# Token rows of a hybrid diffusion step: loaded on SP's queue behind the fourth modulation unit instead of first on ScalarE's queue

## The reference

```python
mod = (jax.nn.silu(cond) @ w_mod + b_mod)[:, None, :]
sh1, sc1, g1, sh2, sc2, g2 = jnp.split(mod, 6, axis=-1)
h = rmsnorm(x, norm1_w) * (1 + sc1) + sh1
(u_in, gate_b, gate_c, q, k, v, g_out, lr_f, lr_b,
 gate_br_conv, gate_br_gla) = jnp.split(h @ w_in, points, axis=-1)
y_conv = gate_b * conv3_rows(gate_c * u_in, conv_w, conv_b, rows, row_len)
y_gla, s_f, s_b = gla_mixer(q, k, v, g_out, lr_f, lr_b, w_decay, b_decay, gla_norm_w, s0_f, s0_b)
merged = (jax.nn.sigmoid(gate_br_conv) * (y_conv @ w_br_conv)
          + jax.nn.sigmoid(gate_br_gla) * (y_gla @ w_br_gla))
x = x + g1 * (merged @ w_out)
h2 = rmsnorm(x, norm2_w) * (1 + sc2) + sh2
x = x + g2 * moe(h2, w_router, b_router, w_gate_e, w_up_e, w_down_e, w_gate_s, w_up_s, w_down_s)
```

## Time and profile before

| | |
|---|---|
| median of three runs | 1021.3 us |
| lowest, highest | 1020.84, 1022.47 us |
| profiled execution, first to last instruction | 1021.6 us |
| TensorE busy | 929.6 us (91%) |
| VectorE busy | 365.8 us (36%) |
| ScalarE busy | 185.9 us (18%) |
| GpSimd busy | 104.1 us (10%) |
| moved by DMA | 324.25 MB, mean 317 GB/s |

### The profile page before, as it was taken

How to read it: one execution, slowest core, us unless ns; L and a number is a source line. 1 busy time by engine, 2 the same in 40 slices (tenths; PEclk the granted TensorE clock), 3 DMA queues, 4 the chain that set the end, 5 groups by cost and what they waited for, 6 DMA issues and landing times.

```text
span 1021.6 us, 12985 instructions
## 1 busy us (share of the span) xinstructions
PE 929.6 (91%) x4915; PEld 481.5 (47%) x4915; DVE 365.8 (36%) x711; ACT 185.9 (18%) x277; POOL 104.1 (10%) x205
## 2 busy tenths in 40 slices
PE   4899899999999999999999999997998897988785
PEld 0454456677555568644444444442433343433332
DVE  3309613137200325442344333333232233232256
ACT  2140320112001002202222112221111121211111
POOL 2000000000000000020212122121121121111100
PEclk9999899999999999999999999998999999999998
DMA  9745556522363359798999999999999999999994
GB/s 373 266 165 213 193 212 206 182 65 76 110 237 130 108 181 421 311 395 357 363 373 418 419 420 419 421 420 419 420 419 421 423 420 419 420 421 420 422 419 199
DMA packets 82384, 324.25 MB, mean 317 GB/s; under 512 B 10350, under 2 KB 39194, under 8 KB 52368
## 3 DMA queue, kind: packets, MB, share of 16 engines
q1 hardware_dynamic: 66864, 289.43, 71.0%
q0 software_dynamic: 10080, 24.44, 6.1%
q10 hardware_dynamic: 5376, 9.52, 2.6%
HBM read 301.52 MB, written 34.11 MB: 329 GB/s over the span
## 4 chain that ended last, share of the span: by engine, by line
PE 78%; DVE 8%; DMA 5%; issue 5%; ACT 3%; SPq 1%; DVEq 0%; ACTq 0%
PE bank L522 25%; PE bank L1680 18%; PE bank L551 13%; PE bank L1837 4%; PE bank L1824 4%; DMA arena<-expert_rows 3%; DMA arena<-in_w_mod_dram 2%; PE bank L509 2%; PE bank L1744 2%; PE bank L1864 2%; ACT arena L533 1%; PE bank L540 1%; DVE arena L536 1%; PE bank L1665 1%; PE bank L482 1%
## 5 line engine op out<-in xcount | busy, mean ns | idle before, releaser
L522 PE MATMUL bank<-arena 128*32 128x512 f32 (+2 forms) x1536 | 266.0, 613 | 35.6 <-issue 34.6
L1680 PE MATMUL bank<-arena 128*128 128x384 f32 x640 | 211.8, 492 | 4.7 <-DVE arena L1072 4.7
L522 PEld LDWEIGHTS bank<-arena 128*32 128x32 f32 (+2 forms) x1536 | 94.0, 127 | 204.7 <-issue 203.9
L1680 PEld LDWEIGHTS bank<-arena 128*128 128x128 f32 x640 | 121.8, 192 | 97.0 <-issue 9.9
L551 PE MATMUL bank<-arena 128*32 128x512 f32 (+2 forms) x768 | 131.5, 595 | 6.6 <-issue 5.9
L551 PEld LDWEIGHTS bank<-arena 128*32 128x32 f32 (+2 forms) x768 | 44.7, 123 | 70.2 <-issue 70.2
L564 ACT ACTIVATE arena<-arena 128x1024 f32<-128x1024 f32 x36 | 41.3, 1148 | 166.3 <-DVE arena L560 163.7
L556 DVE SCALAR_TENSOR_TENSOR arena<-bank,arena 128x512 f32<-128x512 f32 x36 | 27.0, 751 | 108.0 <-PE bank L551 107.9
L496 POOL DMA_INDIRECT arena<-h_rows,arena x36 | 38.4, 1067 | 240.4 <-issue 124.3
L536 DVE TENSOR_TENSOR arena<-arena,bank 128x256 f32<-128x256 f32 x36 | 21.8, 606 | 113.5 <-ACT arena L533 113.5
L533 ACT ACTIVATE arena<-bank 128x256 f32<-128x256 f32 x36 | 22.3, 619 | 204.6 <-PE bank L522 204.6
(11 more groups left out here) (246 smaller groups left out, 713.6 us busy)
## 6 DMA issues: line engine op xcount, KB each, us to landing
arena<-in_w_gate_e_dram SPq DMA_DIRECT2D x64, 1024.0 KB
arena<-in_w_up_e_dram SPq DMA_DIRECT2D x64, 1024.0 KB
arena<-in_w_down_e_dram SPq DMA_DIRECT2D x64, 1024.0 KB
arena<-in_w_mod_dram SPq DMA_DIRECT2D x24, 1024.0 KB, 8.2
arena<-in_w_in_dram SPq DMA_DIRECT2D x22, 1024.0 KB, 5.8
expert_rows<-arena SPq DMA_DIRECT2D x6, 2048.0 KB, 23.6
arena<-expert_rows SPq DMA_DIRECT2D x12, 1024.0 KB, 25.3
arena<-mod_rows_out ACTq DMA_DIRECT2D x4, 1024.0 KB, 8.2
```

Source lines behind the costliest of these rows:

```text
L522: ins = pe.matmul(bank[off:off + width, :], x_T[:, k, off:off + width], w[:, :, k, :], start=(k == 0), stop=(k == KT - 1))
L1680: ins = pe.matmul(ps[:, 0:TOK], w[:, k, P * (n % 2):P * (n % 2) + P], hT[:, k, :], start=(k == 0), stop=(k == KT - 1))
```

## The change

The two DMAs that load x leave ScalarE's program, where they were the first thing, and stand in SP's loop behind the fourth unit. The same semaphore counts them.

```diff
                 sp.dma_start(unit_view(u), unit_source(u)).then_inc(unit_in[n % UNITS], 16)
+                if u == ("mod", 0, 3):
+                    sp.dma_start(xn[:, 0, :], x_prompt[0]).then_inc(S["x_in"], 16)
+                    sp.dma_start(xn[:, 1:3, :], x_sample[0].rearrange("(t p) d -> p t d", p=P)).then_inc(S["x_in"], 16)
...
-            act.dma_start(xn[:, 0, :], x_prompt[0]).then_inc(S["x_in"], 16)
-            act.dma_start(xn[:, 1:3, :], x_sample[0].rearrange("(t p) d -> p t d", p=P)).then_inc(S["x_in"], 16)
             act.wait_ge(S["cond_in"], 32)
             act.wait_ge(S["cond_zeroed"], 1)
```

## The result

The change makes the kernel slower. The changed kernel took 1024.68 us in the median (15 runs, 1022.72 to 1027.44), and the kernel before 1021.96 us (15 runs, 1020.74 to 1024.04, the three known ones among them). The ratio is 1.0032, with a 95% interval of 1.0024 to 1.0041. So the change costs 0.14 to 0.32%, some 1.4 to 3.3 us.

The account below looks back on a forecast made before the run. The prediction took unit 7's landing at 28.8 us, set by DMA bandwidth, as the bound. Terms +0.6 (start), +0.1 (x) and +0.3 (clock) gave +1.0, a median of 1022.3 us, range 1020.7 to 1024.6.

Parts of the forecast that it names:

- What limits the stretch: First 42.64 us: the landing of unit 7 sets the first large projection, and a delay there reaches the end one to one.
- Start of the stream: SP's queue: unit 0, issued at 1.74, flows from about 3.2 us, so all that follows is 0.6 us later.
- The estimate beside it: SP's queue: from the skill's first-byte time, unit 0 would flow at 2.3 us, costing nothing or gaining a little.
- x late: Ahead of unit 7: x lands 9.5 us later, all swallowed but 0.1 us, without a reserve, if TensorE's clock is up.
- The clock: TensorE after the hole before unit 4: lower clock level, then a rise soon after x's rows are ready, costing 0.3 us.
- rival 2: TensorE stays at 1.2 GHz behind the late x; unit 7 starts over 1.4 us behind its landing; chance 0.18.
- cold and half-cold cases: TensorE behind x: lower clock throughout gives +4.3 us, 1025.6; a rise halfway gives about 1023.9 us.
- ScalarE's queue, hidden: ScalarE's later DMA issues start 9.5 us later but finish at 32.0 us, hidden by 0.9 us before the feature copies.
- Rival 3: ScalarE stuck in its queue: router issues take 8.1 us as before, +4.5 us, 1025.8 us; chance 0.08.
- Rival 1: SP's queue flows at once, so nothing shifts or 0.3 us are won: 1021.0 to 1021.3; chance 0.14, shared.
- rival 5: No effect: x does not wait for units 0 to 3 and lands near 10 us, 1021.3; shared chance 0.14.
- Rival 4: Clock luck in later matmul pieces, 2.3 us each: 1019.9 or 1024.6 us; chance 0.05 faster, 0.03 slower.

Follow-up runs that it names:

- experiment 4: Kernel before the change plus six extra 384-column products on TensorE ahead of the first large projection; 1.0036 of the kernel before.
- experiment 6: Changed kernel with x two units later, behind the sixth unit on SP's queue; 1.0074 of the kernel before.
- experiment 2: Changed kernel with x two units earlier, behind the second unit on SP's queue; 1.0018 of the kernel before.
- experiment 3: Changed kernel with x first on SP's queue, ahead of all units and behind the conditioning vectors; 1.0011 of the kernel before.
- experiment 1: Changed kernel with 12 small extra products in TensorE's idle time behind the fourth, fifth and sixth units; 1.0010 of the kernel before.
- experiment 7: Changed kernel with the two conditioning vectors moved to ScalarE's queue, x still behind the fourth unit; 1.0016 of the kernel before.
- experiment 9: Changed kernel with the conditioning vectors on ScalarE's queue and 17 small extra products in TensorE's idle time; 1.0014 of the kernel before.
- experiment 8: Changed kernel with x behind the second unit and the conditioning vectors on ScalarE's queue; 1.0001 of the kernel before.

## Why the prediction was wrong

**What limits the stretch**: right. The landing of unit 7 set the pace before, and where the first large projection was moved by 4 and by 9 us, the end moved with it, within the intervals (experiments 4 and 6).

**Start of the stream, 0.6 us**: right in kind, mis-sized. It measured 1.1 to 1.2 us (experiments 2 and 3), at or just over my upper bound of 1.1. I had let the stream run at its full rate from 3.2 us, from a reading of x's start (2.1 us) that was too early: 253 GB/s over 2 to 3 us is, at 414 GB/s, a start at 2.4. In fact the stream moved 0.09 MB from 3 to 4 us, and its 2.72 to 2.77 MB by 10 us are a full rate from 3.3 to 3.4. The simple account would have been nearer: the first large load is issued 0.92 us later, so all that follows is 0.92 us later. The estimate beside it, a flow from 2.3 us at no cost, fell.

**x late, 0.1 us**: the sum was right. I forecast x at 18.96 and its rows at 26.7; it was 19.57 and 27.3, and the difference is the stream's. With the clock up, unit 7 starts at 29.94 (experiment 1) where the landing alone gives about 30.0 (experiments 2 and 3).

**The clock, 0.3 us**: this is the step that failed. It measured 1.6 to 3.0 us: against experiment 1 the slow array cost 2.96, 1.60 and 1.84 us in three profiles of the changed kernel. I had seen the hole, the lack of a reserve, and the price of the full case, and then wrote "a rise soon after" because the gaps between units 4 and 5 were like those in which the clock had risen. But before, the rise fell into the third unit in a row with such a gap ahead of it (0.52, 0.66 and 0.64 us). After the change only unit 5 has one, and ahead of unit 4 stands the hole. The lower level lasted to 30.7 us or beyond in all three, and unit 7 started 1.5 to 2.2 us behind its landing (30.0), over the 1.4 that I had named for rival 2. Its cold and half-cold cases, to which I gave 0.18 together, are what the profiles show. (The cold case took transposes of 1.74 us, twice 0.87; at the lower level they took 1.54.) The rule of the Trainium skill that I cited (TensorE: Matmul & The Clock Gate, Part 1), that idle gaps bring the throttle back, is borne out by experiment 7 (1.07 us per unit ahead of a gap of 6.54 us, 1.93 behind it), and I gave it too little weight.

**ScalarE's queue, hidden**: right. The two issues that had taken 5.80 and 2.32 us took this:

```profile
28.94 0.81 ACTq L1500 DMA_DIRECT2D arena<-in_b_router_dram  x1
29.78 1.57 ACTq L1501 DMA_DIRECT2D arena<-in_w_router_dram  x1
...
36.32 0.46 ACT L1508 ACTIVATE arena<-bank,arena 128x128 f32<-128x128 f32 x1 [11.64 <-DVEq L1011]
```

ScalarE was done (31.35 us) 5 us before its features were wanted (36.32). Rival 3 fell.

**The sum**: with 1.1 for the start and 1.6 to 3.0 for the clock, the first large projection moves by 2.7 to 4.1 us. The three comparisons gave 1.4 to 3.3. Rival 1 (a free start) fell as well, and with it rival 5: x was used at 19.57, behind units 0 to 3. Rival 4, the luck of the clock later on, is real in single executions (the pieces at 404 and 445 us), but it can't carry a cost that three comparisons of 12 to 15 runs all show. The forecast's unit 7 "at 29.4 to 29.8" should have read 31.5 to 32.2.

## What to carry to other kernels

When a transfer moves from "ready long before" to "just in time", add up the reserve at the slower clock level too: TensorE, idle for the transfer, may run what follows at half speed (1.94 us per unit in place of 1.07), and the work behind it then has nothing to hide in. Issue the first large transfer first: with 0.92 us of small issues ahead of it, the first large projection of this kernel came 0.9 to 1.2 us later (experiment 9 against 1, and 8 against 2). In the whole time this gain was not clear of the spread. And where all bytes are needed before one date, order in a queue has little to win: the best reordering here tied with the kernel before.

## What the runs showed of the hardware

- The large transfers of a queue reached their full rate some 1.5 to 1.7 us after the issue of the first one (an estimate: the bytes moved by 10 us, taken back at 414 GB/s), with or without two loads of 4 KB each (288 packets under 512 B) ahead of it. From 3 to 4 us that looks like 90 against 411 GB/s; it is the same start, 0.92 us apart.
- An array at the upper level came back at the lower one after 6.54 us of idle time (experiment 7), and in experiment 4 after 1.51 us, while gaps of 0.52 to 0.66 us between units did not keep it from rising.
- Until the clock had risen for the first time, its column read 1.00 at both levels, and only the durations (1.94 and 1.07 us per unit) tell them apart. Once it had risen and fallen again, the column read 0.50 (experiment 7, 19 to 32 us).
- Filling idle time of TensorE with products that nobody reads moved the first large projection 2.96, 1.60 and 1.84 us earlier than in the three profiles of the changed kernel.
